# Winograd's seven block products in both column halves of a streamed down projection, with evictions staged by ScalarE and added in device memory

## What is computed

```
    for l in range(DEPTH):
        ...
        h = h + y @ w_o[l]
        n = rmsnorm(h, mlp_norm_w[l])
        h = h + jnp.square(jax.nn.relu(n @ w_up[l])) @ w_down[l]
    return rmsnorm(h, final_norm_w)
```

## Time and profile before

| | |
|---|---|
| time, median of 3 runs (lowest, highest) | 1036.54 us (1036.47, 1037.2) |
| profiled execution: time, span in the profile | 1036.7 us, 1034.9 us |
| TensorE matmul / weight load busy | 98% / 85% |
| VectorE busy | 77% |
| ScalarE busy | 59% |
| GpSimd busy | 9% |
| DMA, mean over the span | 184 GB/s, 190.8 MB moved |
| granted TensorE clock | 0.998 of full speed |

### The profile page before, as it was taken

The page is one execution under the profiler, slowest core; times in us unless marked ns, Lnnn a source line. Parts: engine busy times, 40 slices in busy tenths (PEclk is TensorE's granted clock), DMA queues, the critical chain, the costliest instruction groups (busy, mean ns, idle before and its releaser), DMA issues.

```text
span 1034.9 us, 14187 instructions
## 1 busy us (share of the span) xinstructions
PE 1018.4 (98%) x5547; PEld 881.3 (85%) x5547; DVE 794.0 (77%) x1086; ACT 613.1 (59%) x872; POOL 88.4 (9%) x151
## 2 busy tenths in 40 slices
PE   8999999999999998999999999999999999999997
PEld 7889999888887887888888888888888888888885
DVE  4655886988866479769968967976995996897594
ACT  4655855877764576546556645645664665564433
POOL 2134200732200000000000000000000000000002
PEclk9999999999999999999999999999999999999999
DMA  9576672243236546656666666666666666566553
GB/s 333 184 200 192 206 254 103 100 148 120 82 124 202 163 128 178 210 181 202 201 194 201 189 196 197 203 204 182 203 196 193 203 200 197 180 204 197 202 190 136
DMA packets 182798, 190.84 MB, mean 184 GB/s; under 512 B 9206, under 2 KB 145100, under 8 KB 182348
## 3 DMA queue, kind: packets, MB, share of 16 engines
q1 hardware_dynamic: 182300, 189.41, 58.2%
q10 hardware_dynamic: 432, 0.52, 0.1%
HBM read 187.82 MB, written 2.10 MB: 184 GB/s over the span
## 4 chain that ended last, share of the span: by engine, by line
PE 90%; DVE 6%; ACT 2%; issue 1%; DMA 0%; DVEq 0%; ACTq 0%
PE ps L2007 19%; PE ps L2075 12%; PE ps L2011 10%; PE ps L2082 6%; PE ps L1565 4%; PE ps L1566 4%; PE ps L2049 4%; PE ps L1569 4%; PE ps L2056 4%; PE ps L2050 4%; PE ps L1979 2%; PE ps L1856 2%; PE ps L1857 1%; PE ps L1860 1%; PE ps L1840 1%
## 5 line engine op out<-in xcount | busy, mean ns | idle before, releaser
L979 DVE TENSOR_TENSOR low<-raw,high 128x2048 fp32r<-128x2048 f32 x120 | 259.7, 2165 | 87.8 <-ACT high L826 86.9
L826 ACT ACTIVATE high<-raw 128x2048 fp32r<-128x2048 f32 x120 | 217.4, 1811 | 98.7 <-DMA raw<-in_w_up 75.7
L2007 PE MATMUL ps<-xT,high 128*128 128x512 f32 x896 | 212.9, 390 | 2.7 <-DVE hid L1377 2.7
L2007 PEld LDWEIGHTS ps<-xT,high 128*128 128x128 f32 x896 | 168.0, 188 | 39.1 <-DVE hid L1377 3.6
L979 DVE TENSOR_TENSOR w_lo<-raw,w_hi 128x1024 fp32r<-128x1024 f32 (+4 forms) x79 | 129.5, 1645 | 67.0 <-ACT w_hi L632 66.2
L632 ACT ACTIVATE w_hi<-raw 128x1024 fp32r<-128x1024 f32 (+3 forms) x75 | 104.1, 1391 | 64.6 <-PE ps L1569 40.9
L2075 PE MATMUL ps<-high,hidT 128*128 128x512 f32 x544 | 135.1, 390 | 0.0
L2011 PEld LDWEIGHTS ps<-xT,low 128*128 128x128 f32 x896 | 114.9, 191 | 4.4
L2075 PEld LDWEIGHTS ps<-high,hidT 128*128 128x128 f32 x544 | 100.4, 188 | 19.7
L2011 PE MATMUL ps<-xT,low 128*128 128x256 f32 x896 | 116.2, 283 | 0.0
L2082 PE MATMUL ps<-low,hidT 128*128 128x512 f32 x272 | 72.7, 389 | 0.0
(11 more groups left out here) (367 smaller groups left out, 1887.2 us busy)
## 6 DMA issues: line engine op xcount, KB each, us to landing
raw<-in_w_up SPq DMA_DIRECT2D x64, 1024.0 KB, 6.4
raw<-in_w_down SPq DMA_DIRECT2D x36, 1024.0 KB, 5.2
raw<-in_w_down SPq DMA_DIRECT2D x56, 512.0 KB, 4.7
raw<-in_w_o SPq DMA_DIRECT2D x16, 1024.0 KB, 5.2
raw<-in_w_in SPq DMA_DIRECT2D x8, 1024.0 KB, 5.3
raw<-in_w_in SPq DMA_DIRECT2D x8, 816.0 KB, 4.4
raw<-in_w_in SPq DMA_DIRECT2D x6, 832.0 KB, 8.6
raw<-in_mla_w_uq SPq DMA_DIRECT2D x12, 256.0 KB, 4.4
```

The costliest lines, as they stand in the source:

```text
L826: act.activation(high4[:, n % RAW, c0:2048], raw[:, n % RAW, c0:2048], ACT.Copy).then_inc(done, 1)
L979: return dve.tensor_tensor(dst, src, high.bitcast(F32), ALU.subtract)
L2007: pe.matmul(ps[:, 0, :].rearrange("p (c t) -> p c t", c=2), high4[:, s, P * k:P * k + P], xT[:, :, k, :], start=k == 0, stop=False)
```

## The change

1. Both column halves are made with seven products: `down_quad` runs for all eight i. `down_half` stays for the last group alone.
2. Two of the four weight sums no longer come from VectorE. SP loads two weight blocks straight into `t_sum` (256 KB each) beside 768 KB of the chunk into `raw`, and GpSimd then issues two loads of 256 KB with an accumulating DMA that add a third block onto both. VectorE makes the last two sums. The same holds for every one of the 56 down chunks (before, weight sums were made for 28).
3. The seven banks are copied by ScalarE into `stage`, and GpSimd issues DMAs that add `stage` onto a buffer in device memory (plain copies the first time for each half): 14 times in all. The signs of the hidden sums change so that all these are additions; two hidden sums are made by one instruction.
4. After the loop the two halves' sums are loaded back (`whole`) and merged by VectorE, ahead of the last four chunks on SP's queue.

In the changed file `load_quad` is at L450 (SP), `add_block` and `add_products` at L615 and L625 (GpSimd), `products_out` at L911 (ScalarE), `weight_sums` and `merge` at L1385 and L1502 (VectorE).

```diff
+            def load_quad(g, i):
+                n, s, half, k = down_at(g, i), 8 * (g - 1) + i, i // 4, 2 * (i % 4)
+                place_free(n)
+                if s:
+                    sp.wait_ge(sum_in, 32 * s)
+                left, right = [slice(1024 * half + 512 * c, 1024 * half + 512 * c + 512) for c in range(2)]
+                for b, (row, cols) in enumerate(((k, left), (k + 1, right))):
+                    sp.dma_start(t_sum[:, s % 2, 512 * b:512 * b + 512], dn[:, g - 1, row, cols]).then_inc(sum_in, 16)
+                dst = raw[:, n % RAW, :].rearrange("p (b n) -> p b n", b=4)
+                sp.dma_start(dst[:, 1:3, :], dn[:, g - 1, k:k + 2, left]).then_inc(raw_in[n % RAW], 16)
+                sp.dma_start(dst[:, 3, :], dn[:, g - 1, k + 1, right]).then_inc(raw_in[n % RAW], 16)
...
             for j in range(8):
+                if j == 4:
+                    for half in range(2):
+                        sp.wait_ge(stage_in, 32 * (2 * G - 3 + half))
+                        if half:
+                            sp.wait_ge(back, 16)
+                        sp.wait_ge(w_used, spent(down_at(G - 1, 7)))
+                        sp.dma_start(whole[:, half, :, :], sums[:, half, :, :]).then_inc(back, 16)
                 load_down(down_at(G, j), G - 1, 2 * (j % 4), j // 4)
...
+            def add_block(g, i):
+                n, s, half, k = down_at(g, i), 8 * (g - 1) + i, i // 4, 2 * (i % 4)
+                pool.wait_ge(sum_in, 32 * (s + 1))
+                if s:
+                    pool.wait_ge(sum_both, 32 * s)
+                src = dn[:, g - 1, k, 1024 * half + 512:1024 * half + 1024]
+                for b in range(2):
+                    pool.dma_start(t_sum[:, s % 2, 512 * b:512 * b + 512], src, accum_op=ALU.add).then_inc(sum_both, 16)
+
+            def add_products(g, half):
+                pool.wait_ge(prod_out, 7 * (2 * (g - 1) + half + 1))
+                for banks in (slice(0, 4), slice(4, 7)):
+                    if g == 1:
+                        pool.dma_start(sums[:, half, banks, :], stage[:, banks, :]).then_inc(stage_in, 16)
+                    else:
+                        pool.dma_start(sums[:, half, banks, :], stage[:, banks, :], accum_op=ALU.add).then_inc(stage_in, 16)
+
+            add_block(1, 0)
+            for g in range(1, G):
+                for i in range(8):
+                    if i == 0 and g > 1:
+                        add_products(g - 1, 1)
+                    if i == 4:
+                        add_products(g, 0)
+                    if i < 7:
+                        add_block(g, i + 1)
+                    elif g < G - 1:
+                        add_block(g + 1, 0)
+            add_products(G - 1, 1)
...
+            def products_out(g, half): 
+                m = 2 * (g - 1) + half
+                act.wait_ge(w_used, spent(down_at(g, 4 * half + 3)))
+                if m:
+                    act.wait_ge(stage_in, 32 * m)
+                for b in range(1, 8):
+                    act.activation(stage[:, b - 1, :], bank(b), ACT.Copy).then_inc(prod_out, 1)
...
             def weight_sums(g, i):
+                dve.wait_ge(sum_both, 32 * (s + 1))
-                dve.tensor_tensor(o[:, 0:2, :], r[:, 0:1, :].broadcast_to((P, 2, 512)), r[:, 1:4:2, :], ALU.subtract).then_inc(sum_ok, 1)
-                dve.tensor_tensor(o[:, 2, :], r[:, 3, :], o[:, 0, :], ALU.subtract).then_inc(sum_ok, 1)
+                dve.tensor_tensor(o[:, 2, :], o[:, 0, :], r[:, 3, :], ALU.add).then_inc(sum_ok, 1)
...
+            def merge(half):
+                dve.wait_ge(back, 16 * (half + 1))
+                for dst, x, y, op in ((1, 0, 1, ALU.add), (0, 0, 5, ALU.add), (6, 6, 0, ALU.subtract), (0, 4, 0, ALU.subtract),
+                                      (2, 0, 2, ALU.add), (3, 3, 6, ALU.subtract), (6, 6, 4, ALU.add)):
+                    combine(half, dst, x, y, op)
+                for n, q in enumerate((1, 2, 3, 6)):
+                    t, c0 = n // 2, 1024 * half + 512 * (n % 2)
+                    o = h_sb[:, t, c0:c0 + 512]
+                    dve.scalar_tensor_tensor(out=o, in0=whole[:, half, q, :], scalar=r1[:, t:t + 1], in1=o, op0=ALU.mult, op1=ALU.add)\
+                        .then_inc(merged, 1)
...
             for g in range(1, G):
                 for i in range(8):
                     up_block(g, i)
-                    if i < 4:
-                        down_quad(g, i)
-                    else:
-                        down_half(g, i, 2048, i == 4, i == 7, half_t)
+                    down_quad(g, i)
```

More of the change, by code:

```diff
@@ L242, in build @@
         assert e <= R_AT
-        sink2, e = seq(C_END, ("sink2", [P, D], F32))
+        sink2, e = seq(A_AT + 3 * P + 4 * 3 * 2048, ("sink2", [P, D], F32))
         assert e <= Q_AT
-        hid, acc, T_AT = seq(A_AT, ("hid", [P, 8, T], F32), ("acc", [P, TT, 1024], F32))
+        T_AT = A_AT + 3 * P
         t_low, t_high, e = seq(T_AT, ("t_low", [P, 2, 2048], F32R), ("t_high", [P, 2, 2048], F32R))
+        t_sum, e = seq(T_AT, ("t_sum", [P, 2, 2048], F32))
+        sink3, e = seq(T_AT, ("sink3", [P, 1024], F32))
+        whole, e = seq(T_AT, ("whole", [P, 2, 7, 512], F32))
+        hid, acc, e = seq(T_AT + 4 * 4 * 2048, ("hid", [P, 8, T], F32), ("acc", [P, 1024], F32))
         assert e <= Q_AT
-        t_sum, e = seq(T_AT, ("t_sum", [P, 2, 2048], F32))
-        acc7, e = seq(Q_AT + 4 * TT * D, ("acc7", [P, 7, 512], F32))
+        stage, e = seq(Q_AT + 4 * TT * D, ("stage", [P, 7, 512], F32))
         assert e <= nc.sbuf_usable_end
+        sums = nc.dram_tensor("product_sums", (P, 2, 7, 512), F32, kind="Internal").ap()
         fw, e = seq(X_AT, ("fw", [P, D], F32))
@@ L895, in _ @@
                 for i in range(8):
+                    if i == 0 and g > 1:
+                        products_out(g - 1, 1)
+                    if i == 4:
+                        products_out(g, 0)
                     if (g, i) == (1, 0):
@@ L1478, in _, with combine @@
-            dve.wait_ge(half_out, 2 * (G - 1))
-            for t in range(TT):
-                merge(t, 1024, D, acc[:, t, :])
-            for j in range(4, 6):
-                down_weights_lo(G, j)
-            dve.wait_ge(merged, 6)
+            def combine(half, dst, x, y, op):
+                w = whole[:, half, :, :]
+                link(dve.tensor_tensor(w[:, dst, :], w[:, x, :], w[:, y, :], op))
+            def merge(half):
[8 more added lines that the diff above has]
+                        .then_inc(merged, 1)
@@ L1484, in _ @@
+            hidden_parts(G - 1, 3)
+            for j in range(2, 4):
+                down_weights_lo(G, j)
+            merge(0)
+            down_weights_lo(G, 4)
+            merge(1)
+            down_weights_lo(G, 5)
+            dve.wait_ge(merged, 8)
             last_down()
@@ L2052, in down_quad, with down_half @@
                     if b == 1:
-                        pe.wait_ge(dn_lo, 8 * (g - 1) + p + 1)
+                        pe.wait_ge(dn_lo, s + 1)
                     if b == 5:
                         pe.wait_ge(sum_lo, s + 1)
-                    m = pe.matmul(bank(b), left[b](0), right[b](1), start=False, stop=p == 3)
-                m.then_inc(w_used, 1)
-            def down_half(g, i, base, start, stop, done):
-                n, p = down_at(g, i), i % 4
+                    last = pe.matmul(bank(b), left[b](0), right[b](1), start=False, stop=p == 3)
+                last.then_inc(w_used, 1)
+            def down_half(i, base, start, stop):
+                g, n, p = G, down_at(G, i), i % 4
                 w = n % RAW
```

147 lines of the change are left out of this document (52 added, 95 removed).

## The result

The changed kernel takes **1256.74 us** (median of 4 runs, 1251.21 to 1262.85) where the kernel before takes 1036.51: **1.213 times** the time, 95% interval 1.209 to 1.216. The forecast was 1201 us. The profiled execution took 1258.4 us, its span 1256.4.

What follows compares the result with a forecast made beforehand. It took TensorE to bound the kernel, other engines hiding behind it unless cover fails. Terms −16.5 + 129 + 12 + 25 + 14.5 = +164 on 1036.7 us gave 1201 us; own range 1150 to 1260, 1090 to 1310 with most rivals.

Steps and rivals of the forecast that it cites:

- −16.5 us for TensorE: In the loop, 28 right-half pieces become seven-product pieces, each block going from 11.01 to 10.42 us: −16.5 us.
- (a): Block behind the staged products: its accumulating loads queue behind them on GpSimd, additions at twice a copy's price; 7.2 us late.
- (b): Block after that: VectorE's and ScalarE's chain from the late landing delays the next up block, another 4.5 us each time.
- Ordinary blocks at no cost: Blocks away from the products: VectorE, ScalarE and DMA work was costed at nothing where it has cover.
- the bound T + 10.4: Loads landing within 10.4 us of the end of a half's fourth piece (T) do not delay TensorE; later ones do.
- (c): ScalarE's evictions after the right half lack cover: 4.2 us, six times, 25 us; the left half's are covered.
- (d): Tail: products land late, then the second `whole` and the last chunks' loads and low parts run late: +14.5 us.
- ScalarE and VectorE at nothing on average: Neither engine's total exceeds 10.4 us per block on average, so their added work was costed at nothing where covered.
- the plain price: Rival: an addition by DMA costs no more than a copy; 1107 us, chance 0.22.
- three transfers: Rival: an addition by DMA costs three transfers or more, or GpSimd's DMAs start slowly; 1290 us, chance 0.25.
- GpSimd's DMAs are slow to start: Alternative within the 1290 us rival: ten microseconds of start per DMA would add as much; chance 0.25 shared.
- Volume only: Rival: only DMA volume bounds, 12.8 us for each of 56 blocks; 1168 us, sharing the forecast's chance of 0.47.

Runs made afterwards that it cites:

- x2: Changed kernel with the staged products' additions made plain copies of the same bytes; only the last group's products reach the output: 1193.07 us.
- x6: Changed kernel with GpSimd's accumulating loads onto `t_sum` made plain copies, so weight sums lack a block: 1202.64 us.
- x1: Changed kernel with the products' additions kept in place but carrying 64 bytes a row, most of the products' sum left out: 1156.37 us.
- x13: Changed kernel with x10 and x1 together: three slots and 64-byte product additions, all accumulating loads kept: 1066.24 us.
- x9: Changed kernel with x4 and x1 together: VectorE makes all weight sums and product additions move 64 bytes a row: 1066.82 us.
- x4: Changed kernel without accumulating loads: SP loads whole chunks, VectorE makes all weight sums in all 56 blocks, staged products stay: 1108.83 us.
- x10: Changed kernel with a third slot for `t_sum` and `t_low`, loads and additions one block earlier, same bytes: 1143.80 us.

## Why the prediction was right, and what its steps got wrong

The sign held, and so did the mechanism behind the products; 1256.7 lies in the range (1090 to 1310). The time is 56 us above the number, though, and only 3 us inside the forecast's own range (1150 to 1260), and some terms erred in opposite directions. By steps:

- **−16.5 us for TensorE**: blocks without a wait are 10.3 us. It holds, and is buried.
- **(a) 7.2 us late: the mechanism held, the size did not.** Blocks (g,1) and (g,5) are 22.1 and 22.0 us long, 11.7 over, not 7.2. The terms, from the chain: the evictions end at T + 7.8 instead of T + 4.4 (the step took ScalarE to be free at T, but it still owes a chunk's high part and `t_high`); from there to the landing 20.2 us instead of 17.7. Of these, the transfer was right (15.4 us from the first packet, 15.1 taken, and in the packets SP has a share of 0.14 to 0.20 beside the products, a fifth taken); the start was 4.8 us and not 2.6. The price of an addition, the term with the widest bounds, was right at twice a copy (x2, x6). One figure beside the sum does not follow from the rows: with half of the engines 12.1 us become 24.2, not "some 19", unless SP's loads end on the way.
- **(b) another 4.5 us**: the following blocks are 12.9 and 13.4 us long, 2.5 and 3.0 over. The chain from landing to up block is 10.2 us (taken: 10.5), but TensorE came out of the late piece later than L + 6.0: the piece ended at 629.5, 8.3 us after the landing, in part because it ran at the lower clock. (a) and (b) together are 14.2 and 14.6 us a place instead of 11.7; some 2.7 × 11 = 30 us of the 56 (the terms that follow bring the rest, with group 1, whose round was longer than forecast too).
- **Ordinary blocks at no cost was the step that failed.** The prediction derived the bound T + 10.4 and applied it only behind products. Blocks (g,4) and (g,7) are 3.5 and 0.7 us over, about 25 us over six rounds, and this understates it, since a late block gives its followers time. x1 shows it with almost no products: the round is 104.1 us, and three slots bring it to 88.4 (x13). The same rows gave it: two fixed times of 2.6 us, two transfers of 0.52 MB at 390 GB/s, one of them doubled (1.3 + 2.7), and an issue of about 1 us are 10.2 us on an idle queue, at the bound with nothing to spare; the chain in x1 took 15.0.
- **(c) 4.2 us, six times**: the next (g,0) is 12.9 us, 2.5 over, while x13 (no burst) has 1.1 over at (g,4) and 2.3 at (g,0). So the cover is thin on both sides, and the size was taken too large on one and at nothing on the other; together about as predicted, which is luck. TensorE's waits for evictions sum to 28.2 us.
- **(d) +14.5 in the tail**: from the last piece of the loop to the end it is 68.8 us against 51.5, +17.3. The products landed at T + 19.8 instead of T + 16.4.
- **ScalarE and VectorE at nothing on average**: wrong where it counts. The means are below 10.4 us a block, but the ring in x13 takes 11.56 where hidden sums are made. x9 stands 30 us over before with this, the evictions and the tail, with its DMA engines at 0.65. For x13, as far over, the runs don't part the ring from its full DMA engines.

Loop and tail add up: the loop is 204 us longer, against 149.5 forecast, the tail 17.3 against 14.5. What the runs take back, in order: 100 us with the products' additions (x1), 90 more with a third slot (x13), and 30 remain. The terms are not independent: VectorE's sums with products in a burst (x4) already return 148 of the 190.

Of the rivals, the plain price (1107) and three transfers (1290) are both refuted by x2, which gives two. That GpSimd's DMAs are slow to start was right in part: 4.8 us. *Volume only* (1168) is refuted for the changed kernel by x10, which is 113 us faster with the same bytes; x10 itself has full DMA engines (1.02), though x13 is 78 us faster with engines nearly as full (0.98).

The rule of the Trainium skill ("Collectives: The Full Stack", section on the bandwidth ceiling) that an addition's two source reads halve the rate agrees: 100 against 50 us for 21.8 MB. So does the other one, of turns between queues ("DMA: Bandwidth & Descriptors", section on queues, rings and completion order), in its main point. In the burst followed above, from 612 to 618 us, GpSimd's queue moved 245 packets with data and SP's 247, though from 612 to 614 GpSimd's had 6 KB each and SP's 2 KB, and GpSimd's queue held 0.85 of the engines. The other bursts look alike, and in x4 512-byte packets of SP's took turns too (64 and 64 in 532 to 534 us). The Trainium skill has several descriptors to a turn; in these packets it is one for one. The 20 to 22 us that chunks wait beside the products in x4 and x10 fit this. No run varied the size of the rows, so what other sizes would bring is not shown.

## What to carry to other kernels

Work moved from a busy engine to a DMA is free only if its whole chain (slot free, load, landing, issue, addition, landing) fits between two uses of its slot; work that chain out for the ordinary iteration too, and give it one more slot before judging it. A queue that runs in order hands its burst on to whatever stands next, so before spreading a burst see that its buffer is free in time: look at who waits for the last piece. And a mean below the pace of the bounding engine is no slack where two engines hand work back and forth within a block.

## What the hardware showed that was not expected

TensorE's clock falls during the stalls. Windows of the changed kernel behind the burst above (the clock is the third number from the end):

```profile
612.00:614.00 2.00, 1.10 (x5) 0.56 (x3) 0.00 (x0) 0.00 (x0) 0.00 (x0) 1.00 1.03 236
616.00:618.00 2.00, 0.00 (x0) 0.00 (x0) 0.00 (x0) 0.00 (x0) 0.00 (x0) 0.97 1.10 260
618.00:622.00 4.00, 0.00 (x0) 0.00 (x0) 0.69 (x1) 0.78 (x1) 0.27 (x1) 0.50 1.08 317
622.00:628.00 6.00, 4.15 (x10) 3.32 (x11) 5.92 (x7) 3.66 (x4) 1.48 (x2) 0.50 0.96 205
...
632.00:636.00 4.00, 4.00 (x13) 3.17 (x12) 3.97 (x3) 3.90 (x4) 1.76 (x2) 0.63 0.83 253
```

TensorE ran dry at about 613 us at its full 2.4 GHz (1.00); from about 618 it was granted 1.2 GHz (0.50), and its first matmuls after the wait still ran so, as did part of the next up block, which took 5.52 us instead of 3.64. A stall is therefore paid twice. For the same 5463 matmuls TensorE was busy 1052.8 us here and 1015.6 in x13:

```profile
PE 1015.6 (96%) x5463; PEld 869.2 (82%) x5463; DVE 807.6 (76%) x1060; ACT 693.8 (65%) x1026; POOL 214.3 (20%) x291
```

Those 37 us are about the most that the lower clock adds to the end (x13's own clock was 0.991 in the mean), and some of it lies beside other waits; no run took the clock's part out by itself. Nothing in the forecast stood for it.

Second, three slots let the DMA engines carry 264 GB/s at a share of 1.02, and the kernel with two slots 224 at 0.88: 255 to 259 GB/s when full with this mix (224 / 0.88 and 264 / 1.02), below the 308 that the loop before works out to, where nothing is added. In these windows 29% of the bytes are on GpSimd's queue, nearly all of them added, and these cost twice; x9, with next to none, comes to 299 (194 / 0.65).
